# Moving the second modulation's slots and turn into the up loop, and cutting the down product's sums into pieces

## The chip, the cores and the metric

The kernel runs on one core of a Trainium2 chip. All numbers are float32. The metric is the device time of one execution in microseconds (us); the median of the runs counts. Engines: TensorE (PE in the profile, PEld its weight loads), VectorE (DVE), ScalarE (ACT), GpSimd (POOL) and SyncE (SP), which here issues nearly all DMAs.

## The reference, cut to what matters

Two transformer blocks run one after the other on 512 tokens of width 1024. The change lies in the first block's feed-forward part and in the modulation of the second block:

```
def conv_ffn(h, w_up, conv_w, conv_b, w_down, rows):
    u = h @ w_up                                  # 512 x 5632
    u = conv2d_grid(u, conv_w, rows) + conv_b     # 3 x 3, per channel, on an 8 x 64 grid
    gate, val = jnp.split(u, 2, axis=-1)
    return (jax.nn.silu(gate) * val) @ w_down     # 2816 -> 1024
...
x = x + g2 * conv_ffn(h, ...)                     # end of block one
...
m_lat = jax.nn.silu(c) @ w_mod[l] + b_mod[l]      # block two: sh1, sc1, g1, sh2, sc2, g2
m_ctx = jax.nn.silu(c_ctx) @ w_mod[l] + b_mod[l]
```

## The kernel before

Activations lie feature-major, 128 features on the partitions and the tokens along the free dimension. The feed-forward part is one block of instructions per engine (`ffn_stage`), each engine's list written out by hand; engines wait on semaphores only.

**Up.** `SevenUp` makes the 22 hidden tiles (`KF`). Each tile m has two rows of features: row 0 the gate, row 1 the value. The product of a tile is done as a two-by-two block product with seven instead of eight partial products (`do_p1` to `do_p7`), each 4 steps of 256 columns. A float32 step is two records in the trace, so a period has 56 records (line 2091). The weight sums s1 to s4 of the next tile are made by GpSimd (lines 2023 to 2039), the four sums of the activations t1 to t4 once by VectorE. Intermediate results go through PSUM banks: ScalarE keeps copies (`keep_a`, `keep_u`, `keep_v`, lines 2142 to 2154) and writes quarter c21 (line 2160), VectorE adds c11, c12 and c22 (line 2170) into a padded window. Then the 3 x 3 convolution: of the nine taps per row ScalarE and GpSimd take the first three (`OWN = 3`; ScalarE multiplies, lines 2066 and 2071, GpSimd adds in `join`, line 2048, four joins for a tile, through one buffer for each row), and VectorE the other twelve operations (`taps`, line 2201), which accumulate in banks 0 and 1. ScalarE's SiLU (line 2164) and VectorE's `gate` (line 2207) give the hidden tile and raise `made`. VectorE works two tiles behind TensorE: in period p it does the gate of tile p-3 and the taps of tile p-2.

**Down.** `SevenDown` does four pairs of output tiles with the same seven products, 11 steps of 256 columns each (line 1681, 22 records). Its activation sums t1 to t4 (lines 1666 to 1677) run over half of all hidden tiles at once. GpSimd makes the weight sums of pair 0 (lines 1646 to 1663), VectorE those of the later pairs. `add_...` (line 1730) adds a bank to the residual x. The products one, six, seven and four of a pair share one bank: an addition lies between each and the next. The weights come in quarters `w_down`, 4 for each pair.

**Second modulation.** `SecondMod` multiplies the first 8 slots of `w_mod` (1 MB each, `ada2`) with the vectors `c32` (`rows_by_product`, line 2239, 16 records each), copies the rows out (`take_rows`, ScalarE, line 2245), turns them to the partitions by 32 tiny products (`turn`, line 2251) and adds the bias (`add`, VectorE, lines 2260 to 2268). Slots 0 to 2 come before the up loop, 3 to 7 behind its last product. Slots 6 and 7 lie in memory of their own.

**Weights.** One stream of tiles (`order_of_use`) goes through a ring of `RING = 4` slots. SyncE sends tile n when tile n-4 is free, strictly in order (`send_weights`, line 309). An up tile is free after its fourth product and its fourth weight sum.

Of the kernel before, what the change touches and what calls it, by code (L numbers as in the profile page):

```python
# [45 lines left out]
MOD_APART = 6  # L46
# [1552 lines left out]
class SevenDown:  # L1599
# [9 lines left out]
    def __init__(self, k, before, rhs, gate, x, t_at, t4_at, s_at):  # L1609
# [5 lines left out]
        self.t1, self.t2, self.t3, self.t4 = wide(t_at), wide(t_at + n * c), self.b12, wide(t4_at)  # L1615
        self.s1, self.s2, self.s4 = (narrow(s_at + n * P * i) for i in range(3))
# [48 lines left out]
    def make_t1(self, dve):  # L1665
        dve.tensor_tensor(self.t1, self.b12, self.b11, SUB).then_inc(self.t_made, 1)

    def make_t2(self, dve):
        dve.wait_ge(self.t_made, self.old + 1)
        dve.tensor_tensor(self.t2, self.b22, self.t1, SUB).then_inc(self.t_made, 1)  # L1670
# [4 lines left out]
    def make_t4(self, dve):  # L1675
        dve.wait_ge(self.t_made, self.old + 3)
        dve.tensor_tensor(self.t4, self.b21, self.t2, SUB).then_inc(self.t_made, 1)

    def product(self, pe, bank, w, rhs, first, last, done):
# [10 lines left out]
    def do_p2(self, pe, p):  # L1690
        self.landed(pe, p, 1)
        if p:
            pe.wait_ge(self.z_added, self.old + p)
        self.product(pe, self.Z, self.weights(p, 1), self.b21, True, True, self.p2)
# [7 lines left out]
    def do_p4(self, pe, p):  # L1702
        pe.wait_ge(self.t_made, self.old + 4)
        pe.wait_ge(self.v_added, self.old + p + 1)
        self.landed(pe, p, 3)
        self.product(pe, self.X[p % 2], self.weights(p, 3), self.t4, False, True, self.p4)

    def do_p5(self, pe, p):
        pe.wait_ge(self.s1_made, self.old + p + 1)
        pe.wait_ge(self.t_made, self.old + 1)  # L1710
# [4 lines left out]
    def do_p6(self, pe, p):  # L1715
        pe.wait_ge(self.s2_made, self.old + p + 1)
        pe.wait_ge(self.t_made, self.old + 2)
# [3 lines left out]
    def do_p7(self, pe, p):  # L1721
        pe.wait_ge(self.s3_made, self.old + p + 1)
        pe.wait_ge(self.t_made, self.old + 3)
# [233 lines left out]
class SevenUp:  # L1957
# [3 lines left out]
    OWN = 3  # L1961
    OPS = 2 * (9 - OWN)
# [78 lines left out]
    def join(self, pool, m, row, i):  # L2041

        n = 2 * (i - 1) + 1 - row
        pool.wait_ge(self.own, 2 * self.OWN * m + self.own_number(row, i))
        if i > 1:
            pool.wait_ge(self.joined, 2 * (self.OWN - 1) * m + n - 1)
        q = self.q[:, m % 2, row]
        pool.tensor_tensor(q, q, self.term[1 - row], ADD).then_inc(self.joined, 1)  # L2048

# [4 lines left out]
    def own_tap(self, act, m, row, i):  # L2054

        before = self.joined, 2 * (self.OWN - 1) * m + 2 * (i - 2) + 2 - row
# [130 lines left out]
    def taps(self, dve, m, first, end):  # L2187
        for j in range(first, end):
            i, row = self.OWN + j // 2, j % 2
            a = self.acc(row).rearrange("p (r c) -> p r c", r=ROWS)  # L2190
            if j < 2:
# [4 lines left out]
                dve.wait_ge(self.joined, 2 * (self.OWN - 1) * m + 2 * (self.OWN - 1) - row)  # L2196
                base = self.q[:, m % 2, row]
            else:
                dve.wait_ge(self.tap, (self.OPS - 2) * m + j - 1)
# [10 lines left out]
class SecondMod:  # L2210

    BANKS, TURNED = (5, 7, 2, 3), 4

    def __init__(self, k, rows, c32, apart):
        self.k, self.rows, self.c32, self.apart = k, rows, c32, apart
        self.apart_landed = k.sem("mod2_apart_landed")
        self.mm, self.rows_done, self.turned, self.added, self.ready = (k.sem("mod2_" + n) for n in ("mm", "rows", "turned", "added", "c32"))
        for g in range(MOD_APART):
            k.freed[k.number("ada2", g)] = [(self.mm, g + 1)]

    def load_apart(self, sp):
        for w, g in zip(self.apart, range(MOD_APART, 8)):
            sp.dma_start(w, self.k.d["ada2"][g]).then_inc(self.apart_landed, 16)

    def rows_by_product(self, pe, g):
        k = self.k
        if g < MOD_APART:
            n = k.number("ada2", g)
            k.weights_ready(pe, n)
            w = k.slot(n)  # L2230
        else:
            pe.wait_ge(self.apart_landed, 16 * (8 - MOD_APART))
            w = self.apart[g - MOD_APART]
        w = w.rearrange("p (k m) -> p k m", k=KD)
        if g == 0:
            pe.wait_ge(self.ready, 1)
        for kt in range(KD):
# [383 lines left out]
def ffn_stage(k, norm2, x1, gain, shift, h, hidden, up_places, down_args, mod, norm, context, proj):  # L2621
# [9 lines left out]
    with nc.Block("ffn_up") as block:  # L2631
        @block.sync
        def _(sp):
            k.send_weights(sp, k.number("w_up", 8))
            mod.load_apart(sp)
# [35 lines left out]
        def _(pe):  # L2671
# [8 lines left out]
            for m in range(KF):  # L2680
# [26 lines left out]
            down.do_p3(pe, 0)  # L2707
            down.do_p5(pe, 0)
            down.do_p6(pe, 0)
            down.do_p7(pe, 0)  # L2710
            down.do_p4(pe, 0)
            for p in pairs[1:]:
                if p == 1:
                    pe.wait_ge(mod.added, 1)
# [32 lines left out]
        def _(act):  # L2747
# [4 lines left out]
            for p in range(KF + 3):  # L2752
# [12 lines left out]
                if 1 <= p <= KF:  # L2765
                    up.own_tap(act, p - 1, 0, 2)
# [22 lines left out]
        def _(dve):  # L2789
# [7 lines left out]
            for p in range(KF + 3):  # L2797
# [6 lines left out]
                if 1 <= p <= KF:  # L2804
                    up.c12(dve, p - 1)
                if 2 <= p < KF + 2:
# [1511 lines left out]
```

## Time and profile before

| | |
|---|---|
| runs | 1891.51, 1892.02, 1896.76 us; median 1892.02 |
| profiled execution | 1900.21 us, span 1898.6 us |
| TensorE busy | 1732.2 us (91%) |
| VectorE, ScalarE, GpSimd busy | 958.8, 513.1, 398.9 us |
| mean granted clock of TensorE | 0.958 of 2.4 GHz |
| up loop and down products in the trace | 491.3 to 761.1 us, and 765.6 to 917.9 us |

Times in the rows are us from the start of the span. Records of TensorE are pipelined; a gap is an idle time, and in brackets stands what ended it. A granted clock of 1.00 is 2.4 GHz, of 0.50 is 1.2 GHz.

### The profile page before, as it was taken

To read this page: it belongs to the slowest core of one execution; us is meant where nothing else is said; L and a number is where in the kernel's file an instruction comes from. 1 tells how busy PE (TensorE), PEld (TensorE's weight loads), DVE (VectorE), ACT (ScalarE), POOL (GpSimd) and SP (SyncE) were. 2 spreads that over 40 slices of the span, in tenths; PEclk is the share of its full clock that TensorE was granted. 3 is DMA by queue.
4 is the path that set the end of the run, shared out by engine and by line. 5 is a ranking of instruction groups with operands and counts; after the bars stand their busy time and mean duration, and the time that the engine had idled before them with its cause. 6 is when DMAs were issued, how large, how long until landed. Compare 5 with 4: busy or idle time off the path is not lost. (4 is left out here: it accounts for less than half of the span.)

```text
span 1898.6 us, 29839 instructions
## 1 busy us (share of the span) xinstructions
PE 1732.2 (91%) x12382; PEld 1156.2 (61%) x12382; DVE 958.8 (50%) x1605; ACT 513.1 (27%) x973; POOL 398.9 (21%) x404
## 2 busy tenths in 40 slices
PE   7999988789999999899999998999979988978887
PEld 3554487778788888788888887744443323323332
DVE  1775885557488888823588888633130010000113
ACT  4223553341355545201211112620031011110101
POOL 0000017600588887400111110100010000000000
PEclk9999999999999999899999999999979989989998
DMA  9453034213432222322584323205389999999994
GB/s 356 177 208 124 17 89 100 56 38 144 155 124 81 86 89 90 114 92 91 187 326 157 116 89 106 78 31 224 131 313 419 426 426 425 426 426 426 425 422 197
DMA packets 80537, 380.03 MB, mean 200 GB/s; under 512 B 34464, under 2 KB 37536, under 8 KB 54672
## 3 DMA queue, kind: packets, MB, share of 16 engines
q1 hardware_dynamic: 70000, 350.03, 47.6%
q0 software_dynamic: 7104, 26.68, 3.8%
q8 instruction: 100, 1.64, 0.4%
q10 hardware_dynamic: 3296, 1.38, 0.3%
q14 instruction: 37, 0.30, 0.1%
HBM read 364.09 MB, written 19.92 MB: 202 GB/s over the span
## 5 line engine op out<-in xcount | busy, mean ns | idle before, releaser
L3947 PE MATMUL psum<-mem 128*64 128x512 f32 x1504 | 361.8, 638 | 23.2 <-DMA mem<-in_w_upe 10.4
L2091 PE MATMUL psum<-mem 128*128 128x256 f32 x1232 | 268.8, 380 | 3.8 <-ACT mem L378 2.7
L3947 PEld LDWEIGHTS psum<-mem 128*64 128x64 f32 x1504 | 116.0, 146 | 249.1 <-issue 242.4
L2091 PEld LDWEIGHTS psum<-mem 128*128 128x128 f32 x1232 | 233.5, 190 | 39.2 <-ACT mem L378 3.2
L3053 PE MATMUL psum<-mem 128*128 128x256 f32 x896 | 196.7, 381 | 3.3 <-DVE mem L3234 2.8
L3053 PEld LDWEIGHTS psum<-mem 128*128 128x128 f32 x896 | 169.9, 190 | 30.0 <-issue 5.3
L2201 DVE SCALAR_TENSOR_TENSOR psum<-mem,psum 128x512 f32<-128x512 f32 x220 | 150.2, 746 | 0.0
L1681 PE MATMUL psum<-mem 128*128 128x256 f32 x616 | 138.1, 384 | 5.2 <-issue 4.6
L1681 PEld LDWEIGHTS psum<-mem 128*128 128x128 f32 x616 | 117.4, 192 | 24.3 <-issue 7.0
L4018 DVE TENSOR_TENSOR mem<-mem,psum 128x512 f32<-128x512 f32 x16 | 11.0, 688 | 234.9 <-issue 202.9
L2048 POOL TENSOR_TENSOR mem<-mem 128x512 f32<-128x512 f32 x88 | 111.6, 1280 | 56.8 <-ACT mem L2071 56.8
L699 PE MATMUL psum<-mem 128*128 128x512 f32 (+1 forms) x336 | 119.0, 513 | 0.0
L4030 DVE TENSOR_TENSOR mem<-psum,mem 128x512 f32<-128x512 f32 x32 | 20.6, 686 | 188.7 <-PE psum L3947 181.5
L3926 POOL DMA_INDIRECT y_rows<-mem x15 | 15.1, 1004 | 407.9 <-DVE mem L4030 397.5
L699 PEld LDWEIGHTS psum<-mem 128*128 128x128 f32 x336 | 62.9, 189 | 53.4 <-issue 50.0
L3996 ACT ACTIVATE mem<-psum,mem 128x128 f32<-128x128 f32 x124 | 45.1, 467 | 184.9 <-PE psum L3935 184.9
L3264 DVE SCALAR_TENSOR_TENSOR mem<-mem 128x512 f32<-128x512 f32 x120 | 81.4, 742 | 0.0
L566 ACT ACTIVATE mem<-mem 128x512 f32<-128x512 f32 x28 | 17.5, 629 | 213.3 <-DVE mem L1730 99.5
L4011 ACT ACTIVATE mem<-psum 128x512 f32<-128x512 f32 x16 | 9.6, 599 | 219.3 <-PE psum L3947 219.3
L3935 PE MATMUL psum<-mem 128*128 128x128 f32 x128 | 25.4, 362 | 43.0 <-DMA mem<-h_rows,mem 43.0
L2071 ACT ACTIVATE mem<-mem 128x512 f32<-128x512 f32 x88 | 60.5, 711 | 0.9 <-POOL mem L2048 0.8
L1582 PE MATMUL psum<-mem 128*128 128x512 f32 x128 | 56.9, 597 | 1.8 <-PEq L3496 1.8
(443 smaller groups left out, 2589.8 us busy)
## 6 DMA issues: line engine op xcount, KB each, us to landing
mem<-in_w_upe SPq DMA_DIRECT2D x30, 2048.0 KB, 25.4
mem<-in_w_gate SPq DMA_DIRECT2D x29, 2048.0 KB, 27.4
mem<-in_w_downe SPq DMA_DIRECT2D x27, 2048.0 KB, 31.7
mem<-in_ada SPq DMA_DIRECT2D x32, 1024.0 KB, 6.8
mem<-in_w_up SPq DMA_DIRECT2D x22, 1024.0 KB, 4.9
mem<-in_ada POOLq DMA_DIRECT2D x16, 1024.0 KB, 7.2
mem<-in_w_in_g SPq DMA_DIRECT2D x12, 1024.0 KB, 5.2
mem<-in_w_down SPq DMA_DIRECT2D x16, 704.0 KB, 4.0
```

The lines of the kernel that those rows point to most:

```text
L699: last = pe.matmul(k.bank[b][:, 0:n1 - n0], w[:, kt], h[:, kt, n0:n1], start=kt == 0, stop=kt == KD - 1)
L1582: last = pe.matmul(self.banks[m % len(self.banks)][:, :], w, self.rhs[:, kt], start=i == 0, stop=i == n - 1)
L1681: ins = pe.matmul(self.bank(bank), w[:, i], rhs[:, i], start=first and i == 0, stop=last and i == self.N - 1, skip_group_check=True)
L2048: pool.tensor_tensor(q, q, self.term[1 - row], ADD).then_inc(self.joined, 1)
L2071: act.activation(self.term[1 - row], self.window(m, row, i), ACT.Copy, scale=self.tap_weight(m, row, i)).then_inc(self.own, 1)
L2091: ins = pe.matmul(bank, w[:, i], rhs[:, i], start=first and i == 0, stop=last and i == self.N - 1, skip_group_check=True)
L2201: dve.scalar_tensor_tensor(out=a, in0=self.window(m, row, i), scalar=self.tap_weight(m, row, i), in1=base, op0=MUL, op1=ADD).then_inc(self ...
L3053: ins = pe.matmul(self.bank(bank), w[:, i], rhs[:, i], start=first and i == 0, stop=last and i == self.N - 1, skip_group_check=True)
L3264: ins = dve.scalar_tensor_tensor(out=self.conv[:, ct], in0=src, scalar=w, in1=self.conv[:, ct], op0=MUL, op1=ADD)
L3935: last = pe.transpose(k.bank[kt // 4][:, P * (kt % 4):P * (kt % 4) + P], rows[n % 2][:, P * kt:P * kt + P], k.c("ident"))
L3947: last = pe.matmul(bank[halves[h], :], xs[:, kt, halves[h]], pair[h][0][:, kt, cols], start=kt == 0, stop=kt == tiles - 1, skip_group_chec ...
L3996: ins = act.activation(x[:, kt], k.bank[kt // 4][:, P * (kt % 4):P * (kt % 4) + P], ACT.Identity, bias=shift(kt), scale=gain(kt))
```

## The change

- Slots 3 to 7 of the modulation come in the up loop, ahead of the seventh product of tiles 4, 6, 8, 10 and 12, and their weights in the same place of the ring's stream. The turn comes at tile 14. The row copies are in ScalarE's periods 5, 9 and 13, the addition in VectorE's period 15. All use bank 7 but the first. The separate loads are gone.
- Sums t1 and t2 of the down product are made in 11 pieces each, one per period of the loop (t1 in periods 4 to 14, t2 from 15 on, the last piece behind the loop).
- Tiles 20 and 21 have four own taps instead of three: six joins of GpSimd, ten operations of VectorE.
- GpSimd waits for the four activation sums ahead of its loop. The first weight sum of down pair 0 stands at the end of its period 21, ahead of the joins of tile 21; the other three behind the loop.
- Pair 0 of the down products goes in the order 1, 5, 2, 6, 3, 7, 4 (before 1, 2, 3, 5, 6, 7, 4); the second product starts when hidden tile 20 is made and only its last step waits for tile 21. Places in memory change.

```diff
-MOD_APART = 6
+MOD_LATE = {4: 3, 6: 4, 8: 5, 10: 6, 12: 7}
...
+    def make_t1(self, dve, i, made):
+        dve.wait_ge(made, i + 1)
+        dve.tensor_tensor(self.t1[:, i], self.b12[:, i], self.b11[:, i], SUB).then_inc(self.t1_made, 1)
+
+    def make_t2(self, dve, i, made):
+        dve.wait_ge(made, self.N + i + 1)
+        dve.wait_ge(self.t1_made, i + 1)
+        dve.tensor_tensor(self.t2[:, i], self.b22[:, i], self.t1[:, i], SUB).then_inc(self.t2_made, 1)
...
         for i in range(self.N):
+            if made and i == self.N - 1:
+                pe.wait_ge(made, KF)
...
-    OWN = 3
-    OPS = 2 * (9 - OWN)
+    OWN = [3] * (KF - 2) + [4] * 2
...
-    BANKS, TURNED = (5, 7, 2, 3), 4
+    BANKS, TURNED = (5, 7, 7, 7), 7
...
+        if g in (4, 6):
+            pe.wait_ge(self.rows_done, g // 2)
...
         @block.sync
         def _(sp):
-            k.send_weights(sp, k.number("w_up", 8))
-            mod.load_apart(sp)
...
             up.zero_borders(pool)
+            pool.wait_ge(up.t_made, 4)
...
-                    up.join(pool, p - 1, 1, 2)
-                    up.join(pool, p - 1, 0, 2)
-            pool.wait_ge(mod.mm, 8)
-            down.make_s1(pool, 0)
+                    for i in range(2, up.OWN[p - 1]):
+                        up.join(pool, p - 1, 1, i)
+                        up.join(pool, p - 1, 0, i)
+                if p == KF - 1:
+                    pool.wait_ge(up.p5, KF)
+                    down.make_s1(pool, 0)
+            pool.wait_ge(up.p4, KF)
             down.make_s2(pool, 0)
...
                     up.do_p5(pe, m)
+                if m in MOD_LATE:
+                    mod.rows_by_product(pe, MOD_LATE[m])
+                if m == 14:
+                    mod.turn(pe)
                 up.do_p7(pe, m)
...
-            for g in range(MOD_EARLY, 8):
-                if g == 4:
-                    pe.wait_ge(up.c21_done, KF)
-                mod.rows_by_product(pe, g)
-            pe.wait_ge(up.made, KF // 2)
             pe.wait_ge(up.c11_done, KF)
             down.do_p1(pe, 0)
-            pe.wait_ge(up.c12_done, KF)
-            mod.turn(pe)
-            pe.wait_ge(mod.rows_done, 2)
-            pe.wait_ge(up.made, KF)
-            down.do_p2(pe, 0)
+            pe.wait_ge(up.c21_done, KF)
+            down.do_p5(pe, 0)
+            pe.wait_ge(mod.added, 1)
+            pe.wait_ge(up.made, KF - 1)
+            down.do_p2(pe, 0, up.made)
+            down.do_p6(pe, 0)
             down.do_p3(pe, 0)
-            down.do_p5(pe, 0)
-            down.do_p6(pe, 0)
...
                 if 1 <= p <= KF:
-                    up.own_tap(act, p - 1, 0, 2)
+                    for i in range(2, up.OWN[p - 1]):
+                        if i > 2:
+                            up.own_tap(act, p - 1, 1, i)
+                        up.own_tap(act, p - 1, 0, i)
...
-                if p == KF + 1:
-                    for b in range(1, 4):
-                        mod.take_rows(act, b)
+                if p in (5, 9, 13):
+                    mod.take_rows(act, (p - 1) // 4)
...
+                if 4 <= p < 4 + down.N:
+                    down.make_t1(dve, p - 4, up.made)
+                if p == 15:
+                    mod.add(dve)
+                if p >= 4 + down.N:
+                    down.make_t2(dve, p - 4 - down.N, up.made)
                 if 2 <= p < KF + 2:
                     up.taps(dve, p - 2, 4, 8)
...
-            dve.wait_ge(up.made, KF)
-            dve.wait_ge(up.p3, KF)
-            down.make_t1(dve)
+            down.make_t2(dve, down.N - 1, up.made)
             down.add_a(dve, 0)
-            down.make_t2(dve)
+            down.make_t3(dve)
             down.add_z(dve, 0)
-            down.make_t3(dve)
             down.make_t4(dve)
```

## Rows read from the trace of the kernel before

**Rows 1.** Busy time by engine in one loop period, then clock and DMA
```profile
713.75:725.86 12.11, 12.11 (x57) 10.57 (x56) 9.96 (x16) 6.07 (x11) 9.96 (x9) 1.00 0.24 87
```

**Rows 2.** TensorE behind the up loop: start, length, instruction, count, idle before and releaser
```profile
761.11 4.53 PE L2239 MATMUL psum<-mem 128*32 128x256 f32 x80
765.57 5.02 PE L1681 MATMUL psum<-mem 128*128 128x256 f32 x22
771.30 4.21 PE L2251 MATMUL psum<-mem 128*128 128x2 f32 x32 [0.71 <-ACT mem L2245]
779.45 21.80 PE L1681 MATMUL psum<-mem 128*128 128x256 f32 x88 [3.94 <-issue]
801.91 4.99 PE L1681 MATMUL psum<-mem 128*128 128x256 f32 x22 [0.67 <-DVE mem L1730]
807.53 14.52 PE L1681 MATMUL psum<-mem 128*128 128x256 f32 x66 [0.62 <-issue]
```

**Rows 3.** TensorE in short stretches: length, busy (records), granted clock, DMA share, GB/s
```profile
771.30:774.30 3.00, 3.00 (x27) 1.00 0.45 186
774.40:775.50 1.10, 1.10 (x6) 0.50 0.00 0
779.45:784.50 5.05, 5.05 (x12) 0.50 0.00 0
...
993.15:996.15 3.00, 3.00 (x7) 0.50 0.80 279
...
993.15 17.09 PE L3053 MATMUL psum<-mem 128*128 128x256 f32 x71 [2.61 <-DVE mem L3234]
```

**Rows 4.** VectorE in order of time around the last hidden tile
```profile
770.54 1.42 DVE L2201 SCALAR_TENSOR_TENSOR psum<-mem 128x512 f32<-128x512 f32 x2
771.88 6.67 DVE L2201 SCALAR_TENSOR_TENSOR psum<-mem,psum 128x512 f32<-128x512 f32 x10
778.65 0.69 DVE L2207 TENSOR_TENSOR mem<-psum,mem 128x512 f32<-128x512 f32 x1
779.38 5.16 DVE L1666 TENSOR_TENSOR mem<-mem 128x2816 f32<-128x2816 f32 x1
...
784.86 5.66 DVE L1670 TENSOR_TENSOR mem<-mem 128x2816 f32<-128x2816 f32 x1
...
790.83 3.08 DVE L1673 TENSOR_TENSOR mem<-mem 128x2816 f32<-128x2816 f32 x1
```

**Rows 5.** ScalarE in order of time, same stretch
```profile
767.35 0.72 ACT L2071 ACTIVATE mem<-mem 128x512 f32<-128x512 f32 x1 [0.78 <-POOL mem L2048]
769.09 0.60 ACT L2164 ACTIVATE mem<-psum 128x512 f32<-128x512 f32 x1 [1.02 <-DVE psum L2201]
```

**Rows 6.** GpSimd in order of time, same stretch
```profile
755.80 3.73 POOL L2048 TENSOR_TENSOR mem<-mem 128x512 f32<-128x512 f32 x3 [0.93 <-ACT mem L2071]
762.17 1.76 POOL L2048 TENSOR_TENSOR mem<-mem 128x512 f32<-128x512 f32 x1 [2.63 <-ACT mem L2071]
766.03 3.74 POOL L2048 TENSOR_TENSOR mem<-mem 128x512 f32<-128x512 f32 x3 [2.10 <-ACT mem L2071]
771.60 3.38 POOL L1646 TENSOR_TENSOR mem<-mem 128x1408 f32<-128x1408 f32 x1 [1.83 <-DMA mem<-in_w_down]
```

**Rows 7.** DMAs: SyncE's issue of down tiles, their time to landing, the up tiles
```profile
759.48 4.82 SPq L309 DMA_DIRECT2D mem<-in_w_down  x4
...
DMA to landing us min/median/max: 3.8/4.0/7.5
...
mem<-in_w_up SPq DMA_DIRECT2D x22, 1024.0 KB, 4.9
```

**Rows 8.** Around the loop's begin: TensorE and VectorE in order of time
```profile
491.29 8.71 PE L2091 MATMUL psum<-mem 128*128 128x256 f32 x32 [2.74 <-ACT mem L378]
...
498.42 2.19 DVE L2087 TENSOR_TENSOR mem<-mem 128x1024 f32<-128x1024 f32 x1
...
520.27 2.27 DVE L2201 SCALAR_TENSOR_TENSOR psum<-mem 128x512 f32<-128x512 f32 x2
```

More of the change, by code:

```diff
@@ L1607, with __init__ @@
     X, Z, W, V = (6, 1), 7, 0, 2
-    def __init__(self, k, before, rhs, gate, x, t_at, t4_at, s_at):
+    def __init__(self, k, before, rhs, gate, x, t1_at, t2_at, t4_at, s_at):
         n, c = self.N, self.COLS
@@ L1675, in make_t4, with product @@
     def make_t4(self, dve):
-        dve.wait_ge(self.t_made, self.old + 3)
+        dve.wait_ge(self.t2_made, self.N)
         dve.tensor_tensor(self.t4, self.b21, self.t2, SUB).then_inc(self.t_made, 1)
-    def product(self, pe, bank, w, rhs, first, last, done):
+    def product(self, pe, bank, w, rhs, first, last, done, made=None):
         for i in range(self.N):
+            if made and i == self.N - 1:
+                pe.wait_ge(made, KF)
             ins = pe.matmul(self.bank(bank), w[:, i], rhs[:, i], start=first and i == 0, stop=last and i == self.N - 1, skip_group_check=True)
@@ L1693, in do_p2 @@
             pe.wait_ge(self.z_added, self.old + p)
-        self.product(pe, self.Z, self.weights(p, 1), self.b21, True, True, self.p2)
+        self.product(pe, self.Z, self.weights(p, 1), self.b21, True, True, self.p2, made)
     def do_p3(self, pe, p):
@@ L2043, in join, with joins, ops @@
         n = 2 * (i - 1) + 1 - row
-        pool.wait_ge(self.own, 2 * self.OWN * m + self.own_number(row, i))
+        pool.wait_ge(self.own, 2 * sum(self.OWN[:m]) + self.own_number(row, i))
         if i > 1:
-            pool.wait_ge(self.joined, 2 * (self.OWN - 1) * m + n - 1)
+            pool.wait_ge(self.joined, self.joins(m) + n - 1)
         q = self.q[:, m % 2, row]
         pool.tensor_tensor(q, q, self.term[1 - row], ADD).then_inc(self.joined, 1)
+    def joins(self, m):
+        return 2 * sum(n - 1 for n in self.OWN[:m])
+    def ops(self, m):
+        return 2 * (9 - self.OWN[m])
     def own_number(self, row, i):
@@ L2054, in own_tap @@
     def own_tap(self, act, m, row, i):
-        before = self.joined, 2 * (self.OWN - 1) * m + 2 * (i - 2) + 2 - row
+        before = self.joined, self.joins(m) + 2 * (i - 2) + 2 - row
         if i == 0:
@@ L2195, in taps @@
                     dve.wait_ge(self.c21_done, m + 1)
-                dve.wait_ge(self.joined, 2 * (self.OWN - 1) * m + 2 * (self.OWN - 1) - row)
+                dve.wait_ge(self.joined, self.joins(m + 1) - row)
                 base = self.q[:, m % 2, row]
             else:
-                dve.wait_ge(self.tap, (self.OPS - 2) * m + j - 1)
+                dve.wait_ge(self.tap, sum(self.ops(x) - 2 for x in range(m)) + j - 1)
                 base = a
@@ L2210, with __init__ @@
 class SecondMod:
-    BANKS, TURNED = (5, 7, 2, 3), 4
-    def __init__(self, k, rows, c32, apart):
-        self.k, self.rows, self.c32, self.apart = k, rows, c32, apart
-        self.apart_landed = k.sem("mod2_apart_landed")
+    BANKS, TURNED = (5, 7, 7, 7), 7
+    def __init__(self, k, rows, c32):
+        self.k, self.rows, self.c32 = k, rows, c32
         self.mm, self.rows_done, self.turned, self.added, self.ready = (k.sem("mod2_" + n) for n in ("mm", "rows", "turned", "added", "c32"))
-        for g in range(MOD_APART):
+        for g in range(8):
             k.freed[k.number("ada2", g)] = [(self.mm, g + 1)]
-    def load_apart(self, sp):
-        for w, g in zip(self.apart, range(MOD_APART, 8)):
-            sp.dma_start(w, self.k.d["ada2"][g]).then_inc(self.apart_landed, 16)
     def rows_by_product(self, pe, g):
         k = self.k
[L2227 to L2234, printed above, removed]
+        n = k.number("ada2", g)
+        k.weights_ready(pe, n)
+        w = k.slot(n).rearrange("p (k m) -> p k m", k=KD)
         if g == 0:
             pe.wait_ge(self.ready, 1)
+        if g in (4, 6):
+            pe.wait_ge(self.rows_done, g // 2)
         for kt in range(KD):
@@ L4279, in order_of_use @@
         k.put("w_up", m)
-    for g in range(MOD_EARLY, MOD_APART):
-        k.put("ada2", g)
+        if m in MOD_LATE:
+            k.put("ada2", MOD_LATE[m])
     for g in range(2 * KD):
```

33 lines of the change are left out of this document (13 added, 20 removed).

## The prediction

> **What bounds the kernel now.** I read the busy time of one period of the up loop first, then TensorE's instructions in order of time around the loop's end, the granted clock there, and then VectorE, ScalarE and GpSimd over the same stretch. In a period of 12.11 us TensorE is busy all 12.11 at full clock, VectorE and GpSimd 9.96 each [rows 1]. So inside the loop TensorE alone sets the pace, and any product put there is paid in full, while 2.1 us of VectorE and GpSimd are free. Behind the loop it is the reverse. The last up product ends at 761.1; TensorE then has 4.53 us of modulation products, the first down product, a turn of 4.21 us and an idle of 3.94 us, and goes on at 779.45, when VectorE has made the last hidden tile [rows 2, 4]. VectorE goes from the last taps of tile 20 into those of tile 21 without a gap, 770.54 to 778.6, and then its gate. Two things more are lost: the granted clock is at its lower level (1.2 GHz) from the end of the turn to about 784.5, and the chain through the banks leaves 0.67 and 0.62 us [rows 2, 3]. The fourth product of pair 0 ends at 807.53 + 14.52/3 = 812.4, the mark for all that follows: pair 1 needs its slots, and behind it TensorE is busy again. From 761.1 to the mark is 51.3 us. Seven down products at 4.8 us (14.52/3) are 33.6, the slots 4.5, the turn 3.5 at full clock (27 of its 32 records in 3.00 us at the upper level [rows 3]) and 0.7 more at the lower, idle 4.65, 2.6 lost in the second down product (12 records in 5.05 us at the lower level [rows 3]), 1.3 in the two gaps: 50.9, which closes to within 0.4.
>
> **What moves into the loop.** Five slots (80 records, 4.53 us) and the turn (3.5 us) go between the products of periods 4 to 14, where TensorE has no gap: 8.0 us later at the loop's end. They are not saved, only moved. Their DMAs join the ring of four slots; a 1 MB tile is asked for a period or more before its use, against 4.9 us to landing [rows 7], so nothing. The two loads apart go away, also nothing. ScalarE's three copies of rows (0.6 us each) and VectorE's four small operations of the addition (0.2 us each, behind the taps in period 15) lie in free time. The waits of slots 4 and 6 on those copies are met a period early. The clock in the turn is open: before, the turn together with the 0.71 us idle ahead of it ended at the lower level [rows 2, 3]. In the loop dense products stand on both sides. Zero, or the 1.5 us that an idle of 2.61 us costs elsewhere (3.00 us of products at the lower level) [rows 3]. I take zero, since 0.71 of idle is missing.
>
> **The sums in pieces.** Sums one and two cost VectorE 5.16 and 5.66 us behind the loop, beside GpSimd; the third, alone, 3.08 for as many elements [rows 4]. A piece is a eleventh: 0.3 to 0.5 us, one per period, in the 2.1 us that are free. Gain for VectorE about 10 us, but before only the last hidden tile and not sum one stood ahead of the second product, so TensorE gets little of it. What stays behind the last tile are pieces 9 and 10 of sum two, 0.5 each.
> The Trainium skill (GPSIMD Engine Reference, section Specifications) says that GpSimd's SBUF interfaces are shared with VectorE, and that they contend when a VectorE instruction has two SBUF inputs. The trace agrees: 5.16 against 3.08 us, and 2.27 against 1.42 us for the pair of taps that read only SBUF [rows 4, 8]. By it every piece is 0.5 and the pair of tile 21 costs 2.27, since the weight sums of GpSimd now run beside them; without it the sum below would be 1.3 us lower.
>
> **The tail, in the times of before (the 8.0 us added at the end).** Tiles 20 and 21 get a fourth tap pair from ScalarE and GpSimd, so VectorE has ten taps, not twelve, for each: 2 x 1.33 us less. But GpSimd works strictly in order, and three things now stand in front of the last joins.
> GpSimd: joins of tile 20 ended at 759.5; two more at 1.25 (3.74/3): 762.0. Then comes the first weight sum of the down product. It reads a tile in the slot of the last up tile; that slot is free at 759.48, when SyncE sends [rows 7], and with 4.0 us to landing the sum begins at 763.5 and ends 3.38 later, at 766.9 [rows 6, 7]. Behind it wait all joins of tile 21, which before ran from 762.17 to 769.8. ScalarE's 0.71 us terms fit between joins of the other row, so six joins of 1.25: 774.4.
> ScalarE: the SiLU of tile 20 now stands behind the last own tap of tile 21, and that waits for a join (771.9). So 771.9 + 0.7 + 0.6 = 773.2 for the SiLU, which before ran at 769.09 [rows 5], and hidden tile 20 is made at 774.0 instead of 770.5.
> VectorE: taps of tile 21 from 774.45 instead of 770.54: 2.27 + 8 x 0.667 + a piece 0.4 = 8.0, gate and SiLU 0.8: last hidden tile at 783.2, before 779.3 [rows 4]. Two pieces 1.0 and the first addition 0.47: 784.7.
> TensorE: first product 761.1 to 765.9. The fifth waits for the weight sum: 766.9 to 771.7 (1.0 lost). The second waits for hidden tile 20: 774.05, ten of its eleven steps by 778.5 (2.3 lost). Its last step waits until 783.2, and the sixth starts at 784.7 (4.7 + 1.1 lost). Sixth, third, seventh 14.4; one gap 0.6 (the third product now lies over the other); fourth 4.8. That is 804.5.
> The clock: an idle of 2.61 us between dense products put 3.00 us of products at the lower level, 1.5 lost; the one before the second product lost 2.6 [rows 2, 3]. With 4.7 us idle here, between those: 2.3. Mark at 806.8, and with 8.0 at 814.8: 2.4 us later than 812.4. GpSimd's later sums (second, fourth, third from 774.4, 3.2 each) end at 784, ahead of products six, three and seven.
> The Trainium skill (TensorE: Matmul & The Clock Gate, section on HAM oscillation) says that an idle of TensorE between dense stretches returns the clock to half, and that each next stretch begins cold. The trace agrees in 2.61 us [rows 3]. By it this is the rule against the change: two waits, of 2.3 and 4.7 us, stand where one of 3.94 stood. If the first also cost 1.5, the sum would be 3.6 us later.
> The new wait of GpSimd for the four sums of the up product ahead of the loop holds its next weight sums back, to at most 500.6, when the fourth is made (498.42 + 2.19) [rows 8]. The sixth product of tile 1 comes four products of 1.73 us (12.11/7) after 500.6, at 507.5. Nothing; nor is there a gain, as products fill 491.3 to 500.0 in one stretch [rows 8].
>
> **Sum.** 8.0 + (806.8 - 812.4) = +2.4 us, on the profiled execution 1900.2 + 2.4 = 1902.6. The profiled execution is 8.2 above the median of the runs; the difference carries over: 1892.0 + 2.4 = 1894.4. A change below 0.3% (5.7 us) can't be told from none. Bounds of this mechanism: without the clock loss and with the faster rates, 2.3 + 1.3 less (-1.2); with 1.5 for the turn and 1.5 for the first wait, +5.4. Its own range: 1890.8 to 1897.4.
>
> **The rivals.**
> Quick tail. GpSimd's weight sum does not hold up the joins (it fits in the 2.1 us in which GpSimd waited for ScalarE [rows 6]), so the SiLU is not late either. For it speaks that gap, against it that the landing at 763.5 comes two joins late. VectorE then is never idle: hidden tile 20 at 769.6, tile 21 at 777.6; TensorE loses 2.5 + 1.1 us, no clock loss, mark at 798.9 + 8.0 = 806.9: 5.5 faster, 1886.5. A half of it gives 1889.
> Late landing, slower. The down tile behind GpSimd's first sum takes not the median 4.0 but the 7.5 us that is the slowest of sixteen [rows 7]. GpSimd then starts 3.5 later, and joins, SiLU, taps, gate all follow: 2.4 + 3.5 = +5.9, 1897.9; from 7.3 us on it is slower by over 0.3%. For it: the transfer shares its engines with three others only if these are late, and in the new order they have gone a period before; that speaks against it.
> The change moves work and hides nothing. Slots and turn cost 8.0 in the loop and the waits shrink by as much: 1892.0. It differs from the forecast only in how late GpSimd is.
>
> **How the numbers follow.** Forecast mechanism (1890.8 to 1897.4) 0.62; nothing 0.13; quick tail 0.17, of it half past the bound; late landing or a like wait 0.08, of it most past the bound. Faster 0.09, same 0.84, slower 0.07. The range leaves out the outermost tenth at each side: 1886.8 to 1898.0.
>
> **What would show it.** Up loop 8.0 us longer (the period with the turn 15.6). A GpSimd wait for a down tile just behind the loop, 3.4 us of sum, then six joins in a row with VectorE idle 3 to 4 us before the taps of the last tile. TensorE waits of about 1, 2 and 5 us in pair 0, and half clock behind the last. It would be wrong if the last joins end before 771, if the clock falls after the turn and stays down, or if VectorE's free 2.1 us are less than the pieces need, which would stretch every period.

## The result and the profile after

Eight runs of the changed kernel give 1903.50 to 1914.73 us, median 1908.68; eight runs of the kernel before give 1891.51 to 1901.35, median 1897.39. The ratio is 1.0067 with the interval 1.0046 to 1.0087: the change makes the kernel 0.67% slower, 12.7 us by the ratio and 11.3 by the two medians. I had forecast 2.4 us slower, which can't be told from none, and my range ended at 1898.0.

The profiled executions (1914.73 and 1900.21 us) differ by 14.5 us, and I read the difference by marks that both kernels have. S is the start of the eight records of line 590 ahead of the feed-forward part, T0 the first record behind the last up product, M the start of the next spread of line 590, behind the down products:

| | S to T0 | T0 to M | S to M |
|---|---|---|---|
| before | 275.21 | 165.13 | 440.34 |
| after | 287.93 | 165.94 | 453.87 |
| I had forecast | +8.0 | -5.6 | +2.4 |
| measured | +12.7 | +0.8 | +13.5 |

The mark of the prediction, the end of pair 0's fourth product, lies 52.1 us behind T0 (821.29 + 4.84 - 774.06), before 51.3: the same 0.8 more. TensorE of the changed kernel in order of time, from its S to its M, with T0 at 774.06:

```profile
486.13 1.16 PE L590 MATMUL psum<-mem 128*128 128x128 f32 x8 [0.61 <-DVE mem L585]
...
625.67 1.07 PE L2243 MATMUL psum<-mem 128*32 128x256 f32 x16
626.67 24.50 PE L2103 MATMUL psum<-mem 128*128 128x256 f32 x112
651.10 1.07 PE L2243 MATMUL psum<-mem 128*32 128x256 f32 x16
652.10 24.50 PE L2103 MATMUL psum<-mem 128*128 128x256 f32 x112
676.43 4.65 PE L2255 MATMUL psum<-mem 128*128 128x2 f32 x32
680.95 89.08 PE L2103 MATMUL psum<-mem 128*128 128x256 f32 x400
770.50 3.73 PE L2103 MATMUL psum<-mem 128*128 128x256 f32 x16 [0.47 <-ACT mem L2166]
774.06 4.92 PE L1686 MATMUL psum<-mem 128*128 128x256 f32 x22
779.92 5.01 PE L1686 MATMUL psum<-mem 128*128 128x256 f32 x22 [0.94 <-issue]
786.99 6.24 PE L1686 MATMUL psum<-mem 128*128 128x256 f32 x20 [2.07 <-issue]
802.72 17.95 PE L1686 MATMUL psum<-mem 128*128 128x256 f32 x68 [9.49 <-DVE mem L2219]
821.29 8.89 PE L1686 MATMUL psum<-mem 128*128 128x256 f32 x40 [0.62 <-issue]
...
940.00 1.05 PE L590 MATMUL psum<-mem 128*128 128x128 f32 x8
```

Two slots lie 25.43 us apart, 1.2 more than two periods of 12.11 [rows 1], and that is the price of one slot. The waits of the tail are 0.94, 2.07 and 9.49 us, where I had forecast 1.0, 2.3 and 4.7 + 1.1. The granted clock in four stretches (length, TensorE busy and records, weight loads, VectorE, ScalarE, GpSimd, clock, DMA share, GB/s). The first holds the last 2.2 us of the turn and the 4.3 us behind it, the last is the period in which the turn stands:

```profile
678.90:685.40 6.50, 6.50 (x22) 5.60 (x22) 0.42 (x2) 0.66 (x2) 2.43 (x2) 0.50 0.00 0
788.00:791.20 3.20, 3.20 (x9) 2.53 (x8) 3.20 (x2) 0.00 (x0) 3.06 (x2) 0.50 0.00 0
802.75:808.45 5.70, 5.70 (x13) 4.18 (x14) 5.70 (x6) 2.68 (x6) 0.00 (x0) 0.50 0.40 126
671.34:690.35 19.01, 19.01 (x90) 16.85 (x89) 10.73 (x17) 5.99 (x11) 11.81 (x10) 0.82 0.16 58
```

The turn lasts from 676.43 to 681.08. Read in steps of a quarter microsecond, the granted clock is at its upper level up to 678.8 and again from 685.6, and at the lower one (1.2 GHz) for 6.8 us between, though TensorE was not idle for a moment: the fall comes some 2.4 us into the turn, not behind it. That period, 19.01 us between the same quarter of two neighbouring tiles, is 6.9 longer than a plain one: some 3.6 for the turn at full clock, as before [rows 2, 3] and in kernel 2 below (3.63), and 3.3 for the clock, about half of the 6.8 us.

VectorE around the last hidden tile, to be read beside [rows 4]:

```profile
787.48 7.14 DVE L2213 SCALAR_TENSOR_TENSOR psum<-mem 128x512 f32<-128x512 f32 x2 [0.59 <-POOL mem L2052]
794.54 1.40 DVE L2213 SCALAR_TENSOR_TENSOR psum<-mem,psum 128x512 f32<-128x512 f32 x2
795.86 2.06 DVE L1673 TENSOR_TENSOR mem<-mem 128x256 f32<-128x256 f32 x1
...
801.98 0.69 DVE L2219 TENSOR_TENSOR mem<-psum,mem 128x512 f32<-128x512 f32 x1
```

and GpSimd in the same stretch, beside [rows 6]:

```profile
776.64 3.18 POOL L1647 TENSOR_TENSOR mem<-mem 128x1408 f32<-128x1408 f32 x1 [1.56 <-DMA mem<-in_w_down]
779.77 7.61 POOL L2052 TENSOR_TENSOR mem<-mem 128x512 f32<-128x512 f32 x6
787.34 3.16 POOL L1654 TENSOR_TENSOR mem<-mem 128x1408 f32<-128x1408 f32 x1
790.64 3.43 POOL L1664 TENSOR_TENSOR mem<-mem 128x1408 f32<-128x1408 f32 x1
794.03 3.60 POOL L1657 TENSOR_TENSOR mem<-mem 128x1408 f32<-128x1408 f32 x1
```

The pair of taps that read only SBUF takes 7.14 us instead of 1.42 [rows 4]. It ends at 794.62, 0.55 us after GpSimd's sum that ran beside it (790.64 + 3.43 = 794.07). The piece of sum two, 0.41 us when alone, ends 0.29 us after the next sum (797.92 against 797.63). The taps that take one input from SBUF and one from a bank are not touched, 1.40 for two beside a running sum. The durations of all taps of the loop (count: least, median, most, in ns) fit: those with an input from a bank never exceed 751, those with two SBUF inputs reach 3657:

```profile
L2213 DVE SCALAR_TENSOR_TENSOR psum<-mem,psum x216: 737/744/751, 522.6 to 801.1; 128x512 f32<-128x512 f32 x108
L2213 DVE SCALAR_TENSOR_TENSOR psum<-mem x44: 746/760/3657, 520.4 to 791.0; 128x512 f32<-128x512 f32 x44
```

Here each tap with both inputs in SBUF is held until GpSimd's running instruction is over, 3.2 to 3.4 us long. The Trainium skill (SBUF — State Buffer, section "SBUF: two separate sides") says that VectorE and GpSimd share a pair of ports by an exclusive lock, held for the whole instruction by the one that starts first. The trace agrees, in 7.14 against 1.42 us. What the prediction had priced by a ratio is in this case not a slower rate but a full stop.

### The profile page after: what moved, and what is told of

Read it like the earlier page. It is cut to its first block and busy times, and to the rows that moved or that the text cites. A ratio compares the mean times of both kernels' runs of the same rounds, so it can differ in the third digit from the quotient of the medians.

```text
span 1913.1 us, 29877 instructions
## 1 busy us (share of the span) xinstructions
PE 1734.2 (91%) x12382; PEld 1159.8 (61%) x12382; DVE 971.9 (51%) x1621; ACT 515.3 (27%) x977; POOL 401.9 (21%) x408
## 5 line engine op out<-in xcount | busy, mean ns | idle before, releaser
L3953 PE MATMUL psum<-mem 128*64 128x512 f32 x1504 | 355.4, 629 | 19.7 <-DMA mem<-in_w_upe 9.0
L2103 PE MATMUL psum<-mem 128*128 128x256 f32 x1232 | 272.6, 383 | 3.9 <-ACT mem L378 2.8
L2103 PEld LDWEIGHTS psum<-mem 128*128 128x128 f32 x1232 | 234.8, 191 | 41.5 <-ACT mem L378 3.3
L3059 PE MATMUL psum<-mem 128*128 128x256 f32 x896 | 197.9, 382 | 4.2 <-DVE mem L3240 3.7
L3059 PEld LDWEIGHTS psum<-mem 128*128 128x128 f32 x896 | 170.8, 191 | 31.2 <-issue 6.2
L1686 PE MATMUL psum<-mem 128*128 128x256 f32 x616 | 140.4, 388 | 13.1 <-DVE mem L2219 9.5
L1686 PEld LDWEIGHTS psum<-mem 128*128 128x128 f32 x616 | 118.6, 194 | 33.5 <-DVE mem L2219 9.9
L2052 POOL TENSOR_TENSOR mem<-mem 128x512 f32<-128x512 f32 x92 | 116.3, 1277 | 60.4 <-ACT mem L2083 60.4
L699 PEld LDWEIGHTS psum<-mem 128*128 128x128 f32 x336 | 62.9, 189 | 53.4 <-issue 50.0
L3941 PEld LDWEIGHTS psum<-mem 128*128 128x128 f32 x128 | 22.3, 203 | 61.3 <-DMA mem<-h_rows,mem 57.5
```

The costliest lines, as they stand in the source:

```text
L699: last = pe.matmul(k.bank[b][:, 0:n1 - n0], w[:, kt], h[:, kt, n0:n1], start=kt == 0, stop=kt == KD - 1)
L2103: ins = pe.matmul(bank, w[:, i], rhs[:, i], start=first and i == 0, stop=last and i == self.N - 1, skip_group_check=True)
L3941: last = pe.transpose(k.bank[kt // 4][:, P * (kt % 4):P * (kt % 4) + P], rows[n % 2][:, P * kt:P * kt + P], k.c("ident"))
L3953: last = pe.matmul(bank[halves[h], :], xs[:, kt, halves[h]], pair[h][0][:, kt, cols], start=kt == 0, stop=kt == tiles - 1, skip_group_chec ...
```

## The experiments

Each is named by its edit; the diffs show the lines that matter, and `...` stands for lines left out. S to T0, T0 to M and the sum against before (440.34) come from the profile of each, the ratio from its runs beside runs of the kernel before on the same chip. The ratio is not the quotient of the two medians: that would be 1.0074 for kernel 1 and 1.0024 for kernel 5. Kernels 1 to 4 ran on one chip, 5 to 8 on a second, 9 on a third, 9 again and 10 on a fourth.

| kernel | S to T0 | T0 to M | S to M | median, of before | ratio |
|---|---|---|---|---|---|
| after | 287.93 | 165.94 | +13.53 | 1908.68, 1897.39 | 1.0067 [1.0046, 1.0087] |
| 1 move only | 287.86 | 169.82 | +17.34 | 1911.14, 1897.19 | 1.0055 [1.0035, 1.0075] |
| 2 pair first | 289.31 | 161.24 | +10.21 | 1906.74, 1897.19 | 1.0036 [1.0019, 1.0054] |
| 3 turn in quarters | 284.07 | 165.53 | +9.26 | 1904.19, 1897.19 | 1.0036 [1.0021, 1.0050] |
| 4 both | 284.07 | 161.90 | +5.63 | 1902.53, 1897.19 | 1.0015 [0.9997, 1.0032] |
| 5 pieces apart | 284.07 | 158.85 | +2.58 | 1903.00, 1898.53 | 1.0030 [1.0013, 1.0046] |
| 6 three taps | 286.13 | 160.59 | +6.38 | 1901.39, 1898.53 | 1.0013 [0.9995, 1.0031] |
| 7 a slot before | 282.86 | 162.39 | +4.91 | 1899.60, 1898.53 | 1.0022 [1.0002, 1.0041] |
| 8 all of these | 282.87 | 158.97 | +1.50 | 1899.73, 1898.53 | 1.0006 [0.9992, 1.0021] |
| 9 tail kept | 279.01 | 161.26 | -0.07 | 1891.96, 1899.36 | 0.9954 [0.9936, 0.9972] |
| 9 again | 276.98 | 155.63 | -7.73 | 1891.44, 1897.48 | 0.9966 [0.9952, 0.9981] |
| 10 sum after | 277.70 | 157.02 | -5.62 | 1891.68, 1897.48 | 0.9964 [0.9947, 0.9980] |

**1. The move only.** The kernel before, with slots 3 to 7 and the turn in the loop and nothing else of the change: sums whole and behind the loop, order 1, 2, 3, 5, 6, 7, 4, three own taps.

```diff
...
+                if m in MOD_LATE:
+                    mod.rows_by_product(pe, MOD_LATE[m])
+                if m == 14:
+                    mod.turn(pe)
                 up.do_p7(pe, m)
...
-            for g in range(MOD_EARLY, 8):
-                if g == 4:
-                    pe.wait_ge(up.c21_done, KF)
-                mod.rows_by_product(pe, g)
```

> The kernel before with one part of the change alone: slots 3 to 7 and the turn in the up loop (ring, banks, row copies and addition as in the change), down product as before. Theory A (what moves into the loop is the main loss: 1.20 us for each slot and 6.9 us for the turn with the clock loss behind it, and the time that it leaves behind the loop was hidden under VectorE's taps anyway): up loop 12.7 us longer than before, stretch from the last up product to the end of pair 0 unchanged at 51 us, so +12.7 us. Theory B (the move costs only the 8.0 us of the prediction and the tail's new order costs the rest): loop +8, total +8.

The loop is 12.65 us longer, as much as in the whole change: the moved products cost that, and the pieces cost the loop nothing. The tail was expected unchanged by theory A and came out 4.7 us longer, and VectorE and GpSimd show why:

```profile
783.90 6.44 DVE L2201 SCALAR_TENSOR_TENSOR psum<-mem 128x512 f32<-128x512 f32 x2
```

```profile
783.07 3.15 POOL L1646 TENSOR_TENSOR mem<-mem 128x1408 f32<-128x1408 f32 x1
786.36 3.41 POOL L1653 TENSOR_TENSOR mem<-mem 128x1408 f32<-128x1408 f32 x1
```

Here too the pair of taps is held, by two weight sums. Before, the first sum waited for a transfer until 771.60, when the pair had been running for 1.06 us, and the pair took 1.42 [rows 4, 6]. With the slots in the loop SyncE begins to send the down tiles 36.9 us ahead of T0 (before, 1.6 us), the sum begins without a wait, and VectorE stands. No edit of the tail is needed to make the collision; the move makes it.

**2. The pair first.** The changed kernel, in which GpSimd does its second weight sum only when the two taps of tile 21 are done. The wait replaces nothing else; all sums stay.

```diff
             pool.wait_ge(up.p4, KF)
+            pool.wait_ge(up.tap, sum(up.ops(x) - 2 for x in range(KF - 1)) + 2)
             down.make_s2(pool, 0)
```

> The changed kernel, where GpSimd makes the last three weight sums of pair 0 only when VectorE has done the first two taps of tile 21. Theory: these two taps read only SBUF and each is held until a running weight sum of 3.2 to 3.4 us ends (7.14 us for the pair instead of 1.42). Then the pair is back at 1.4 us, some of the hold returns in the pieces of sum two, and the last hidden tile comes 4 to 6 us earlier, the end of pair 0 too: 4 to 5 us faster than the changed kernel, +9 to +10 on the kernel before. Rival (the pair is slow for its window or its place in memory): the pair stays at 7 us and the time at +13 to +14.

VectorE in order of time:

```profile
785.33 1.42 DVE L2213 SCALAR_TENSOR_TENSOR psum<-mem 128x512 f32<-128x512 f32 x2 [0.59 <-POOL mem L2052]
...
787.97 2.35 DVE L1673 TENSOR_TENSOR mem<-mem 128x256 f32<-128x256 f32 x1
...
794.99 2.09 DVE L1673 TENSOR_TENSOR mem<-mem 128x256 f32<-128x256 f32 x2
```

The pair is back at 1.42 us and T0 to M 4.7 us shorter. The hold has moved on in part, to the pieces of sum two: 2.35 us, and 2.09 for the last two. The loop is 1.4 longer; its first 32 records took 10.02 us, in the changed kernel 8.62. Two more differences in this loop nearly cancel: only 3.4 us behind the turn are at the lower clock, and TensorE waits once for a copy of ScalarE, which the changed kernel's loop doesn't have:

```profile
708.71 59.11 PE L2103 MATMUL psum<-mem 128*128 128x256 f32 x272 [1.35 <-ACT mem L2166]
```

What made that copy late was not followed up.

**3. The turn in quarters.** The changed kernel with the 32 tiny products eight at a time, at tiles 14 to 17, and the addition in period 18.

```diff
...
-        for m in range(16):
+        for m in range(4 * q, 4 * q + 4):
...
-                if m == 14:
-                    mod.turn(pe)
+                if 14 <= m < 18:
+                    mod.turn(pe, m - 14)
...
-                if p == 15:
+                if p == 18:
                     mod.add(dve)
```

> The changed kernel with the turn cut into four quarters of 4 tiny products at tiles 14 to 17, the addition in period 18. Theory: the turn itself costs 3.6 us wherever it stands in the loop, and the other 3.3 us of its period are the lower clock behind 4.6 us of tiny products. In quarters the granted clock stays at 2.4 GHz: periods 14 to 17 are each about 1.0 us longer, the loop 3 us shorter than in the changed kernel, +10.5 on the kernel before. Rival (the turn's cost is the waits of its weight loads): each quarter costs 1.7 us and nothing is gained.

TensorE in order of time, from the first quarter on:

```profile
675.80 0.95 PE L2256 MATMUL psum<-mem 128*128 128x2 f32 x8
676.61 12.36 PE L2103 MATMUL psum<-mem 128*128 128x256 f32 x56
688.80 0.95 PE L2256 MATMUL psum<-mem 128*128 128x2 f32 x8
```

A quarter costs 0.95 us of its own, 0.9 in the distance of two (13.00 against 12.11), and the 56 records behind it take 12.36 us, as in a plain period: no loss of clock. S to T0 is 3.9 us shorter, of which 0.5 lies in the first products of the loop, whose clock varies between executions; 3.3 are left, the price of the clock.

**4. Both edits.**

> Both edits, the late weight sums and the turn in quarters. The two lie in different stretches, so they add: 7 to 8 us faster than the changed kernel, +6 to +7 on the kernel before. If they don't add, TensorE's waits behind the loop take up what the loop gains.

The two gains add: 284.07 as in 3, 161.90 beside 161.24 in 2. The runs don't tell it from the kernel before any more.

**5. Pieces apart.** Kernel 4 with each piece of sum two one period earlier, and GpSimd's second sum behind piece 9, its fourth and third behind piece 10.

```diff
-                if p >= 4 + down.N:
-                    down.make_t2(dve, p - 4 - down.N, up.made)
+                if 3 + down.N <= p < KF + 2:
+                    down.make_t2(dve, p - 3 - down.N, up.made)
...
-            pool.wait_ge(up.tap, sum(up.ops(x) - 2 for x in range(KF - 1)) + 2)
+            pool.wait_ge(down.t2_made, down.N - 1)
             down.make_s2(pool, 0)
+            pool.wait_ge(down.t2_made, down.N)
             down.make_s4(pool, 0)
```

> The kernel of the two edits together, with the pieces of sum two one period earlier, so that only the last stands behind the last hidden tile, and GpSimd's second weight sum of pair 0 made when piece 9 is done, the fourth and third when piece 10 is done. Theory (a VectorE operation with two SBUF inputs is held until the running GpSimd instruction ends, 2.35 us for a piece of 0.41): no piece and no tap behind the loop is held any more, the last hidden tile comes 2 us earlier and the sixth product 3 to 4 us; total 3 us below the kernel of both edits. Rival (GpSimd's later sums now make products six and three wait): nothing is gained.

**6. Three taps.** Kernel 4 with three own taps for every tile.

```diff
-    OWN = [3] * (KF - 2) + [4] * 2
+    OWN = [3] * KF
```

> The kernel of the two edits together, with three own taps for tiles 20 and 21 as for all others. Theory: the first tap of tile 21 waits for GpSimd's last join and for the SiLU behind the last own tap, so the fourth pair gives VectorE 1.3 us and costs it 2.5 us of start; with three the last hidden tile comes about 1 us earlier. Rival (the fourth pair helps, as the change has it): it comes 1 to 3 us later.

**7. A slot before.** Kernel 4 with slot 3 ahead of the loop.

```diff
-MOD_EARLY = 3
-MOD_LATE = {4: 3, 6: 4, 8: 5, 10: 6, 12: 7}
+MOD_EARLY = 4
+MOD_LATE = {6: 4, 8: 5, 10: 6, 12: 7}
...
-            k.send_weights(sp, k.number("w_up", 3))
+            k.send_weights(sp, k.number("w_up", 2))
```

> The kernel of the two edits together, with slot 3 of the modulation ahead of the up loop instead of at tile 4. Theory: TensorE idles 2.8 us there for ScalarE, so the slot costs nothing, and the loop is 1.2 us shorter; the first products may also escape the lower clock (1.7 us). Rival: its 1 MB delays the first up tile, and the loop begins later by as much.

**8. Edits 5 to 7 together.**

> All three edits on the kernel of both edits. If they add, 5 to 7 us below that kernel and 0 to 2 us below the kernel before: the change would be no loss once its costs are cut, and hardly a gain.

In the stretches 5 and 7 do what was expected (-3.05 us in the tail; -1.21 in the loop, the price of a slot). In 6 the tail is 1.3 shorter, and the loop 2.1 longer by its first 32 records: 10.16 us, in kernel 4 8.1 with a gap of 0.66 among them. Its theory did not hold: the last hidden tile comes no earlier, 23.2 us behind T0 in both; the 1.3 us are the last two pieces of sum two, which take 0.77 instead of 2.09. The runs confirm none of the three: kernel 5 has a median 0.5 us above that of 4, on another chip, and its ratio of 1.0030 says slower than before, though its stretch is but 2.58 us longer; its profiled execution, 1896.79 us, was the fastest of its ten. Kernel 8 is 4.1 us below kernel 4 in the stretch, where 5 to 7 had been expected, and 1.50 above before, where 0 to 2 below had been; its ratio of 1.0006 can't be told from none. So the loss is no longer seen, but repairs of this tail gave no gain.

**9. The tail kept.** What the first eight say: a product in the loop costs its full length and more, and before, there was an idle of 3.94 us behind the loop [rows 2]. So only slots 3 and 4 go into the loop, 5 to 7 behind it, and the turn, two quarters at a time, to the two waits for hidden tiles. Three own taps; sum one in pieces as in the change, sum two whole; all of GpSimd's weight sums behind the pair of taps; pair 0 in the order 1, 2 (ten steps), 5, 2 (the last), 3, 6, 7, 4.

```diff
-MOD_LATE = {4: 3, 6: 4, 8: 5, 10: 6, 12: 7}
+MOD_LATE = {6: 3, 10: 4}
...
+            for g in range(5, 8):
+                if g == 6:
+                    pe.wait_ge(up.c21_done, KF)
+                mod.rows_by_product(pe, g)
             pe.wait_ge(up.c11_done, KF)
             down.do_p1(pe, 0)
-            pe.wait_ge(up.c21_done, KF)
+            pe.wait_ge(up.c12_done, KF - 1)
+            for q in range(2):
+                mod.turn(pe, q)
+            pe.wait_ge(up.made, KF - 1)
+            down.do_p2(pe, 0, range(down.N - 1))
+            for q in range(2, 4):
+                mod.turn(pe, q)
             down.do_p5(pe, 0)
-            pe.wait_ge(mod.added, 1)
-            pe.wait_ge(up.made, KF - 1)
-            down.do_p2(pe, 0, up.made)
+            pe.wait_ge(up.made, KF)
+            down.do_p2(pe, 0, range(down.N - 1, down.N))
+            down.do_p3(pe, 0)
             down.do_p6(pe, 0)
-            down.do_p3(pe, 0)
...
```

> The parts of the change that fill a wait, without those that fill the loop: slots 3 and 4 in the loop (tiles 6 and 10), slots 5 to 7 and the turn (in quarters) behind it, where TensorE waits for VectorE; sum one in pieces in the loop, sum two whole behind it; three own taps; GpSimd's four weight sums behind the first taps of tile 21; order 1, turn, ten steps of 2, turn, 5, last step of 2, 3, 6, 7, 4. Theory: the loop is 2.4 us longer than before; behind it slots 2.7, product one 4.8, turn 3.5, products two and five 9.6 leave TensorE no idle until the last hidden tile at 18.3 us, so the end of pair 0 comes 40 to 44 us behind the last up product instead of 51: 5 to 8 us faster than the kernel before. Rival (the third, sixth and seventh product now wait for weight sums and for sum two, all behind each other): no faster than before.

> The kernel of the wait-filling parts once more, since its profile and its time differ: by the profile the stretch up to the end of the down products is as long as before, by the runs the kernel is 0.46% faster. If the time is right, again 0.3 to 0.6% faster and another profile with a stretch 3 to 5 us shorter; if the first profile is typical, within 0.2% of the kernel before.

In both measurements this kernel is faster than the kernel before: 0.9954 and 0.9966, 8.7 and 6.5 us by the ratio, 7.4 and 6.0 by the medians. Pair 0's fourth product ends 47.4 us behind T0 in the first profile and 41.8 in the second, before 51.3; 40 to 44 had been expected. The two profiles differ by 7.7 us in S to M: 2.0 lie in the first products of the loop (10.12 against 8.09 us), 5.6 behind it, where one has a wait of TensorE of 3.77 us and some 3.4 us at the lower clock behind that, and the other neither. First profile, TensorE, VectorE, GpSimd:

```profile
781.58 5.44 PE L1684 MATMUL psum<-mem 128*128 128x256 f32 x24
790.80 11.47 PE L1684 MATMUL psum<-mem 128*128 128x256 f32 x44 [3.77 <-POOL mem L1664]
...
784.54 3.19 DVE L1673 TENSOR_TENSOR mem<-mem 128x2816 f32<-128x2816 f32 x1
...
784.93 5.81 POOL L1664 TENSOR_TENSOR mem<-mem 128x1408 f32<-128x1408 f32 x1
```

Second profile of the same kernel:

```profile
779.62 15.04 PE L1684 MATMUL psum<-mem 128*128 128x256 f32 x68
...
782.58 5.19 DVE L1673 TENSOR_TENSOR mem<-mem 128x2816 f32<-128x2816 f32 x1
...
781.65 3.17 POOL L1664 TENSOR_TENSOR mem<-mem 128x1408 f32<-128x1408 f32 x1
```

Where VectorE's sum two starts 0.39 us ahead, it takes 3.19 and GpSimd's sum 5.81, ending 3.0 us behind it; where GpSimd starts 0.93 us ahead, its sum takes 3.17 and sum two 5.19. Whichever is first takes no more than alone.

**10. The sum after.** Kernel 9 with sum two held until that weight sum is made.

```diff
         dve.wait_ge(self.t1_made, self.N)
+        dve.wait_ge(self.s4_made, self.old + 1)
```

> The kernel of the wait-filling parts, where VectorE makes sum two only when GpSimd's fourth weight sum is done. There sum two started 0.4 us ahead of that weight sum, which then took 5.81 instead of 3.16 us, and TensorE idled 3.77 us for it. Theory (whichever of the two starts first holds the other for its whole length): the weight sum is back at 3.2 us, the wait at about 1 us, and with the clock kept the end of pair 0 comes 3 to 4 us earlier. Rival (sum two or the third weight sum becomes late for products six and seven): no gain.

Sum two in VectorE's timeline:

```profile
785.29 5.94 DVE L1674 TENSOR_TENSOR mem<-mem 128x2816 f32<-128x2816 f32 x1 [2.33 <-POOL mem L1664]
```

The 3.77 us wait can't occur, but VectorE stands 2.33 us and then meets the next weight sum, which gives TensorE a wait of 1.10 us. In the runs it is no better than kernel 9 (1891.68 beside 1891.44 us). Which case the unprofiled runs of kernel 9 fall into isn't known.

## Why the prediction was wrong

The forecast was 11.1 us too low (13.5 against 2.4 in the traces): 4.7 in the loop, 6.4 in the tail. In the medians a part of the distance lies in the start: I had added to the 1892.02 us of three runs, and eight runs of the kernel before have the median 1897.39. From 1892.02 the measured loss would give 1904.7, still above my 1898.0.

**The step that failed** is the one for VectorE in the tail, "taps of tile 21 from 774.45 instead of 770.54: 2.27 + 8 x 0.667 + a piece 0.4 = 8.0". The pair took 7.14, the piece 2.06: 4.9 and 1.7 us more, 6.6 where 6.4 are missing; the other terms of the tail cancel to 0.2 the other way. I had foreseen that GpSimd's weight sums run beside them, but took the price of a meeting from the pair at 520.27 [rows 8], which met a GpSimd instruction of 1.27 us. The hold lasts until the other's instruction is over, and the weight sums last 3.2 to 3.6. Kernel 2 shows it: with the order changed and all work kept, the pair took 1.42 and the tail was 4.7 us shorter. GpSimd of the kernel before, read beside [rows 4], could have told it:

```profile
778.42 3.17 POOL L1663 TENSOR_TENSOR mem<-mem 128x1408 f32<-128x1408 f32 x1
781.54 6.03 POOL L1656 TENSOR_TENSOR mem<-mem 128x1408 f32<-128x1408 f32 x1
```

Sum one starts at 779.38, 2.2 us before the first of these ends at 781.59: 2.2 + 3.08 are its 5.16 to 0.13. Then GpSimd stands until sum one ends at 784.54 and takes 3.03 more, to 787.57; sum two starts at 784.86 and ends 2.95 behind that. Each is its own length plus what was left of the other, not its length at a slower rate.

**The clock in the turn.** "I take zero, since 0.71 of idle is missing" was wrong: the clock fell within the turn, with no idle around it, and that cost 3.3 us. My upper bound had been 1.5, from an idle. Kernel 3 shows that it is the turn as one stretch: eight tiny products at a time cost no clock. The size varies: in kernel 1's profile the clock was at the lower level for 6.8 us too, in kernel 2's, where the turn took 3.63 us, it fell 0.2 us behind the turn and for 3.4 us, a loss of some 1.7.

**The slots.** 0.9 us each in a series behind the loop [rows 2], 1.20 in the loop: 1.5 us for five. So 16 products with 128 x 32 weights, set between those with 128 x 128, cost 0.3 us more than in a row of their own. I had taken the series' rate. That a product in the loop is paid in full was right, and by kernel 1 the moved work alone makes the loop 12.65 us longer.

**What was right.** Behind T0 the chain up to the pair of taps went as worked out. GpSimd's first weight sum began 2.58 us behind T0 (forecast 2.4), on a wait for a down tile; six joins followed in a row, the SiLU of tile 20 stood at 11.53 (11.5), the pair began at 13.42 (13.35). The first two waits of TensorE were 0.94 and 2.07 (1.0 and 2.3), and the clock was at half behind the second (nine records in 3.20 us), which I had left out of the sum. The trace agrees there with the rule of the Trainium skill that I had weighed (TensorE: Matmul & The Clock Gate, section on HAM oscillation), with two limits: the wait of 0.94 us brought no fall, and behind the 2.07 us the clock fell only some 1.2 us into the product. The cost did not show in the sum, since the second product's last step waited for the last tile anyway. That step started 28.66 us behind T0 instead of 22.1, which is the failed step's 6.6; the wait ahead of it is 9.49 instead of 4.7 and not longer still, as the ten steps before it took 1.7 more at half clock. The pieces did not stretch the periods: the loop of kernel 1, without them, is as long. But they cost more than the 0.3 to 0.5 us that I had given them: sum one's took 0.66 to 1.02, sum two's 0.41 to 2.06 with a median of 1.24, in time of VectorE that was free.

**The rivals.** The quick tail fell, since the first weight sum did hold up the joins. The late landing fell too: the transfer came on time, 1.56 us of wait. "Moves work and hides nothing" is nearest for the tail, which stayed as long as before (+0.8) though slots and turn had left it, but the sum wasn't zero, as the moved work cost 12.7 in the loop and not 8.0. The slower side came from a mechanism that was in my sum, as a term of 2.27 us.

**What stays open.** Why the first products of the loop run now at the full and now at half clock (32 records in 8.1 to 10.2 us over these profiles) was not tried. It moves single profiles by up to 2 us, so stretch and median of one kernel need not agree that closely. Nor is it known what sets how long the clock stays low behind one and the same turn (3.4 to 6.8 us). That kernels 9 and 10 gain by the filled waits and the late sums is argued from their rows; their parts were not run one by one.

## What to carry to other kernels

When two instructions of VectorE and GpSimd can meet, price the meeting for the one that starts second: its own length plus what is left of the first, not a ratio seen elsewhere. First ask which VectorE operations read SBUF twice, then put the long GpSimd sums behind them, and see which one starts first. Work put into a loop without gaps costs its length, some more for each piece set between others (0.3 us for a slot here), and what it does to the clock; before moving it there, look whether the idle times that remain behind the loop can hold it in small parts. And ask what arrives earlier after a move: here earlier weights started the sums that stopped VectorE, with no other edit.

## What the runs showed of the hardware

- The clock can fall with no idle of TensorE. In or just behind 32 products of 2 columns, 3.6 to 4.7 us without a gap, it was at half for 3.4 to 6.8 us (changed kernel, kernels 1 and 2); with sixteen at a time, 1.9 us (kernels 9 and 10), or eight, 0.95 us (kernel 3), it did not fall.
- Even a tiny VectorE operation is held, and it need not read two tensors from SBUF. In period 15 of the changed kernel an operation over 128 x 8 elements stands 1.18 us beside a running join, 0.17 without one (second profile of kernel 9). The one ahead of them with a single input tensor (`TENSOR_SCALAR`) takes 0.56 instead of 0.17 and ends at 695.27, 0.03 behind the join that ran beside it (693.96 + 1.28):

```profile
694.71 0.56 DVE L2267 TENSOR_SCALAR mem<-mem 128x16 f32<-128x16 f32 x1
695.30 1.20 DVE L2270 TENSOR_TENSOR mem<-mem 128x16 f32<-128x16 f32 x1
696.53 1.18 DVE L2272 TENSOR_TENSOR mem<-mem 128x8 f32<-128x8 f32 x1
```

and GpSimd beside it:

```profile
693.96 1.28 POOL L2052 TENSOR_TENSOR mem<-mem 128x512 f32<-128x512 f32 x1 [4.29 <-ACT mem L2083]
695.19 1.27 POOL L2037 TENSOR_TENSOR mem<-mem 128x512 f32<-128x512 f32 x1
696.43 1.26 POOL L2052 TENSOR_TENSOR mem<-mem 128x512 f32<-128x512 f32 x1
```

- The hold goes both ways, and 0.4 us in the start decides who is held: GpSimd's sum took 5.81 us beside sum two, and 3.17 when it was first. Two executions of the same kernel fell to different sides.
